# Two of every eight expert-row dot products through TensorE instead of VectorE

## What is computed

```
def peer(x, w_q, sub_keys, u_tab, v_tab):
    q = (xt @ w_q).reshape(n_tok, PEER_HEADS, 2, D_QHALF)
    sc = einsum("thcd,hckd->thck", q, sub_keys)
    top_s, top_i = top_k(sc, 16)                  # per head and half
    ...                                           # 16 x 16 pairs, best 16 of them
    experts, gates = ...                          # (tokens, 8 heads, 16)
    u = u_tab[experts]                            # 16384 rows of 2048 in each table
    h = einsum("thkd,td->thk", u, x)              # 128 dot products of 2048 per token
    coef = gates * gelu(h)
    return einsum("thk,thkd->td", coef, v_tab[experts])
```

## Time and profile before

| | us |
|---|---|
| median of 3 runs | 3703.89 |
| lowest, highest | 3697.67, 3709.7 |
| profiled execution | 3707.39 |
| its span, first to last instruction | 3705.7 |
| VectorE busy | 2809.0 (76%) |
| GpSimd busy | 2165.9 (58%) |
| TensorE busy | 2132.5 (58%) |
| ScalarE busy | 588.5 (16%) |
| mean granted TensorE clock | 0.769 of 2.4 GHz |
| HBM read | 1103.41 MB, 298 GB/s over the span |

### The profile page before, as it was taken

One profiled execution on the slowest core, in us unless ns is written; L12 is line 12 of the kernel. 1 busy time (PEld: TensorE's weight loads), 2 busy tenths in 40 slices (PEclk: granted clock), 3 DMA queues, 4 the chain that ended last, 5 costly groups with the idle time before them and its releaser, 6 DMA issues. The chain is left out here.

```text
span 3705.7 us, 32338 instructions
## 1 busy us (share of the span) xinstructions
PE 2132.5 (58%) x8985; PEld 1496.3 (40%) x8985; DVE 2809.0 (76%) x3476; ACT 588.5 (16%) x1079; POOL 2165.9 (58%) x1470
## 2 busy tenths in 40 slices
PE   8968890000111489999499998900001113799993
PEld 7855790000111354444297976900001113544441
DVE  4997589898999766666733545898989998666667
ACT  1002430000111430000033543300001113400000
POOL 6794175888777447767400001758787774477774
PEclk9987995555555589999799999955555555799997
DMA  7421447999999569999755334479999995599997
GB/s 242 143 84 62 142 149 306 395 409 381 422 421 419 201 231 410 408 409 403 291 201 183 126 126 148 145 304 392 412 364 418 422 420 220 210 404 407 409 407 299
DMA packets 293725, 1106.71 MB, mean 299 GB/s; under 512 B 21957, under 2 KB 120837, under 8 KB 220677
## 3 DMA queue, kind: packets, MB, share of 16 engines
q0 software_dynamic: 147456, 805.37, 54.4%
q1 hardware_dynamic: 146182, 300.22, 22.5%
HBM read 1103.41 MB, written 2.10 MB: 298 GB/s over the span
## 5 line engine op out<-in xcount | busy, mean ns | idle before, releaser
L1270 DVE SCALAR_TENSOR_TENSOR ring<-ring,x_tok 128x2048 f32<-128x2048 f32 x512 | 1147.7, 2288 | 56.8 <-DMA ring<-in_peer_u,index_now 53.3
L510 POOL DMA_INDIRECT ring<-in_peer_u,index_now x512 | 961.1, 1877 | 329.6 <-DVE ring L1270 152.9
L733 PE MATMUL ps<-all_v,mix 128*128 128x512 f32 x1984 | 851.8, 592 | 0.0
L531 POOL DMA_INDIRECT work<-in_peer_v,index_add x344 | 455.2, 1323 | 321.4 <-DVE x_tok L1294 174.7
L1294 DVE SCALAR_TENSOR_TENSOR x_tok<-work,coef,x_tok 128x1024 f32<-128x1024 f32 x344 | 441.6, 1286 | 240.2 <-DMA work<-in_peer_v,index_add 238.9
L733 PEld LDWEIGHTS ps<-all_v,mix 128*128 128x128 f32 x1984 | 377.0, 190 | 474.5 <-issue 474.5
L717 PE MATMUL ps<-hot,hot 128*128 128x128 f32 x1024 | 229.9, 411 | 568.2 <-ACT hot L928 568.1
L477 POOL TENSOR_TENSOR w_lo<-ring,w_hi 128x2048 fp32r<-128x2048 f32 x34 | 159.1, 4683 | 663.9 <-ACT w_hi L831 663.9
L717 PEld LDWEIGHTS ps<-hot,hot 128*128 128x128 f32 x1024 | 209.8, 311 | 588.5 <-ACT hot L928 588.5
L707 PE MATMUL ps<-ident,coef 128*128 128x128 f32 x4 | 1.9, 474 | 695.2 <-DVE coef L1288 695.2
L1103 DVE TENSOR_TENSOR w_lo<-ring,w_hi 128x2048 fp32r<-128x2048 f32 x78 | 178.8, 2292 | 264.8 <-ACT w_hi L831 264.8
(11 more groups left out here) (171 smaller groups left out, 2878.0 us busy)
## 6 DMA issues: line engine op xcount, KB each, us to landing
all_v<-in_peer_v SPq DMA_DIRECT2D x248, 512.0 KB, 6.7
ring<-in_conv_w_in SPq DMA_DIRECT2D x16, 2048.0 KB, 8.6
ring<-in_peer_w_q SPq DMA_DIRECT2D x16, 2048.0 KB, 8.3
ring<-in_attn_w_kv SPq DMA_DIRECT2D x16, 2048.0 KB, 8.3
ring<-in_conv_w_out SPq DMA_DIRECT2D x8, 2048.0 KB, 7.7
ring<-in_attn_w_q SPq DMA_DIRECT2D x8, 2048.0 KB, 8.4
ring<-in_attn_w_o SPq DMA_DIRECT2D x8, 2048.0 KB, 7.8
ring<-in_peer_u,index_now POOLq DMA_INDIRECT x512, 9.9
```

What stands on the lines that cost most here:

```text
L510: pool.indirect_dma_start(u_tile(s), None, u_tab, bass.IndirectOffsetOnAxis(ap=index_now[:, half, s:s + 1], axis=0)).then_inc(u_row[s], 16)
L531: pool.indirect_dma_start(add_tile(k), None, v_tab, bass.IndirectOffsetOnAxis(ap=index_add[:, half, k % TB, k // TB:k // TB + 1], axis=0)) ...
L733: mm = pe.matmul(ps[:, dense_bank(tb, q), :], mix[tb][:, row, :], tile[:, q * 512 - HALF:(q + 1) * 512 - HALF], start=False, stop=True, sk ...
L1270: dve.scalar_tensor_tensor(out=u_tile(s), in0=u_tile(s), scalar=1.0, in1=x_tok[:, tb, :], op0=ALU.mult, op1=ALU.mult, accum_out=coef[:, tb ...
```

## The change

In each group of eight tiles those in places 3 and 7 (`TURNED`) are no longer multiplied on VectorE. TensorE transposes such a tile in 16 blocks of 128 x 128, in two halves of two banks each (banks 4 to 7); ScalarE copies each half to `u_chan` in SBUF; TensorE then multiplies the 16 transposed blocks with the transposed x of the block (`x_dot`), summed into a 128 x 128 square of bank 2 or 3, whose diagonal holds the dot products; VectorE multiplies the square with the identity and sums (`take_dot`), one group later. `x_dot` is made once per block by 16 transposes and two copies. GpSimd's gather for places 3 and 7 now waits for `u_turned`, the transposes, and for the other six for `u_used` as before. The order of TensorE and ScalarE is rewritten so that the mixes of block 0 and the turned tiles of block 1 alternate; `turn_slots` moves from bank 2 to bank 0; the third v gather waits for the last product, as `x_dot` lies where `more_add` is.

```diff
+TURNED = (3, 7)
 ...
+        x_dot = nc.alloc_sbuf_tensor_at("x_dot", [P, KC, P], F32, offset=x_chan_at + 4 * 2048)
+        u_chan = view(18432, 2, KC // 2, P)
 ...  GpSimd
-                                        pool.wait_ge(u_used, i * (2 * U_RING) + ((base + half) * U_RING + s + 1))
+                                        if s in TURNED:
+                                            pool.wait_ge(u_turned, i * (4 * NT) + ((base + half) * (2 * NT) + 2 * TURNED.index(s) + 2))
+                                        else:
+                                            pool.wait_ge(u_used, i * (2 * ND) + ((base + half) * ND + DOTTED.index(s) + 1))
 ...
+                        if k == 2:
+                            pool.wait_ge(h_steps, 2 + 2 * NT * GROUPS * TB * (layer + 1))
 ...  TensorE
+                def turned_dots(tb, i):
+                    base = (layer * TB + tb) * GROUPS
+                    for e, s in enumerate(TURNED):
+                        n = base * NT + e
+                        pe.wait_ge(u_row[s], i * 16 + (base + 1) * 16)
+                        for h in range(2):
+                            pe.wait_ge(u_taken, i * (2 * NT) + (2 * n + h + 1))
+                            for c in range(KC // 2):
+                                k = h * (KC // 2) + c
+                                mm = pe.transpose(turned_banks(h)[:, c, :], u_tile(s)[:, k * P:(k + 1) * P], ident[:, :])
+                            mm.then_inc(u_turned, 1)
+                        pe.wait_ge(h_taken, i * NT + (n + 1))
+                        for h in range(2):
+                            pe.wait_ge(u_taken, i * (2 * NT) + (2 * n + h + 3))
+                            for c in range(KC // 2):
+                                mm = pe.matmul(ps[:, 2 + e, 0:P], u_chan[:, h, c, :], x_dot[:, h * (KC // 2) + c, :],
+                                               start=(h == 0 and c == 0), stop=(h == 1 and c == KC // 2 - 1), skip_group_check=True)
+                            mm.then_inc(h_steps, 1)
+
+                turn_dot_x(0)
+                with pe.Fori(0, GROUPS) as i:
+                    turned_dots(0, i)
+                turn_dot_x(1)
+                turned_dots(1, 0)
+                turn_slots(0)
+                turned_dots(1, 1)
+                with pe.Fori(0, GROUPS - 2) as i:
+                    mix_pair(0, i)
+                    turned_dots(1, i + 2)
+                with pe.Fori(GROUPS - 2, BATCHES // 2) as i:
+                    mix_pair(0, i)
 ...  ScalarE
+                def take_turned(tb, i):
+                    for e in range(NT):
+                        n = (layer * TB + tb) * GROUPS * NT + e
+                        for h in range(2):
+                            act.wait_ge(u_turned, i * (2 * NT) + (2 * NT + 2 * n + h + 1))
+                            act.wait_ge(h_steps, i * (2 * NT) + (2 * n + h + 1))
+                            act.activation(u_chan[:, h, :, :], turned_banks(h), ACT.Copy).then_inc(u_taken, 1)
 ...
+                take_dot_x(1)
+                take_turned(1, 0)
                 take_slots(0)
                 act.wait_ge(slot_taken, layer * TB + 1)
+                take_turned(1, 1)
+                with act.Fori(0, GROUPS - 2) as i:
+                    weigh_pair(i)
+                    take_turned(1, i + 2)
 ...  VectorE
+                def take_dot(tb, e, steps, slot):
+                    dve.wait_ge(h_steps, steps)
+                    block = ps[:, 2 + e, 0:P]
+                    dve.scalar_tensor_tensor(out=block, in0=block, scalar=1.0, in1=ident[:, :],
+                                             op0=ALU.mult, op1=ALU.mult, accum_out=coef[:, tb, slot]).then_inc(h_taken, 1)
+
                 def dots(tb, first, last):
                     base = (layer * TB + tb) * GROUPS
                     with dve.Fori(first, last) as i:
                         for s in range(U_RING):
-                            dot(tb, s, i * 16 + (base + 1) * 16, bass.ds(i * U_RING + s, 1))
+                            if s in TURNED:
+                                e = TURNED.index(s)
+                                take_dot(tb, e, i * (2 * NT) + (2 * ((base - 1) * NT + e) + 4), bass.ds(i * U_RING + s - U_RING, 1))
+                            else:
+                                dot(tb, s, i * 16 + (base + 1) * 16, bass.ds(i * U_RING + s, 1))
```

More of the change, by code:

```diff
@@ L62, in build @@
     GROUPS = SLOTS // U_RING
+    DOTTED = [s for s in range(U_RING) if s not in TURNED]
+    NT, ND = len(TURNED), len(DOTTED)
     HALF = D // 2
@@ L709, in mix_slots, with mix_pair @@
-                def mix_slots(tb):
+                    pe.transpose(ps[:, 0, 2 * P:3 * P], coef[:, tb, :], ident[:, :]).then_inc(slot_ready, 1)
+                def mix_pair(tb, i):
                     at = (layer * TB + tb) * BATCHES
[L712 to L718, removed]
@@ L720, in peer @@
-                for tb in range(TB):
-                    turn_slots(tb)
-                    mix_slots(tb)
+                    for b in range(2):
+                        pe.wait_ge(hot_ready, i * 2 + (at + b + 1))
+                        pe.wait_ge(mix_taken, i * 2 + (at + b + 1))
+                        for k in range(BATCH):
+                            mm = pe.matmul(ps[:, b, k * P:(k + 1) * P], hot_2[:, b, k, :], hot_1[:, b, k, :], start=True, stop=True)
+                        mm.then_inc(mix_ready, 1)
@@ L724, in peer @@
+                with pe.Fori(0, BATCHES // 2) as i:
+                    mix_pair(1, i)
                 for tb in range(TB):
@@ L930, in weigh_hot, with take_dot_x, weigh_pair @@
                     last.then_inc(hot_ready, 1)
-                exp_of(layer, 0, 1)
-                for half in range(2):
-                    exp_of(layer, 1, half)
+                def take_dot_x(tb):
+                    for h in range(2):
+                        act.wait_ge(dot_x_turned, 2 * (layer * TB + tb) + h + 1)
+                        act.activation(x_dot[:, h * (KC // 2):(h + 1) * (KC // 2), :], turned_banks(h), ACT.Copy).then_inc(dot_x_taken, 1)
+                def take_turned(tb, i):
+                    for e in range(NT):
+                        n = (layer * TB + tb) * GROUPS * NT + e
+                        for h in range(2):
+                            act.wait_ge(u_turned, i * (2 * NT) + (2 * NT + 2 * n + h + 1))
+                            act.sem_inc(act_tick, 1)
+                            act.wait_ge(h_steps, i * (2 * NT) + (2 * n + h + 1))
+                            act.sem_inc(act_tick, 1)
+                            act.activation(u_chan[:, h, :, :], turned_banks(h), ACT.Copy).then_inc(u_taken, 1)
+                take_dot_x(0)
+                exp_of(layer, 0, 1)
+                with act.Fori(0, GROUPS // 2) as i:
+                    take_turned(0, i)
+                exp_of(layer, 1, 0)
+                with act.Fori(GROUPS // 2, GROUPS) as i:
+                    take_turned(0, i)
+                exp_of(layer, 1, 1)
                 act.wait_ge(route[layer], part_at(1, 1) + PART_STEPS)
+                take_dot_x(1)
+                take_turned(1, 0)
                 take_slots(0)
                 act.wait_ge(slot_taken, layer * TB + 1)
+                take_turned(1, 1)
                 made = layer * TB * 2 * BATCHES
-                with act.Fori(0, BATCHES // 2) as i:
+                def weigh_pair(i):
                     for b in range(2):
@@ L946, in peer @@
                     take_mix(0, i, 1)
+                with act.Fori(0, GROUPS - 2) as i:
+                    weigh_pair(i)
+                    take_turned(1, i + 2)
+                with act.Fori(GROUPS - 2, BATCHES // 2) as i:
+                    weigh_pair(i)
                 take_slots(1)
@@ L1277, in dots, with last_dot, opening_dots @@
                         for s in range(U_RING):
-                            dot(tb, s, i * 16 + (base + 1) * 16, bass.ds(i * U_RING + s, 1))
-                def opening_dots(first, last):
+                            if s in TURNED:
[3 more added lines that the diff above has]
+                                dot(tb, s, i * 16 + (base + 1) * 16, bass.ds(i * U_RING + s, 1))
+                def last_dot(tb, e):
+                    s = TURNED[e]
+                    take_dot(tb, e, 2 * (((layer * TB + tb + 1) * GROUPS - 1) * NT + e) + 4, slice(SLOTS - U_RING + s, SLOTS - U_RING + s + 1))
+                def opening_dots(tb, first, last):
                     for s in range(first, last):
-                        dot(0, s, (layer * TB * GROUPS + 1) * 16, slice(s, s + 1))
+                        if s not in TURNED:
+                            dot(tb, s, ((layer * TB + tb) * GROUPS + 1) * 16, slice(s, s + 1))
+                        elif tb:
+                            last_dot(tb - 1, TURNED.index(s))
                 def weights(tb):
@@ L1325, in peer @@
                         dots(1, 2 + b // 2, 3 + b // 2)
+                for e in range(NT):
+                    last_dot(1, e)
```

35 lines of the change are left out of this document (25 added, 10 removed).

## The result

The changed kernel takes 3663.07 us, median of 4 runs (3659.05 to 3666.84); the kernel before took 3706.8 beside it. The ratio is 0.9877, with a 95% interval of 0.9859 to 0.9895: 1.2% faster. The forecast was 3673, the range of the forecast alone 3656 to 3692, and with the rivals 3648 to 3732. The measured difference is -43.7 us where -31 was forecast.

A forecast was written before the change was run, and what follows sets the result against it. Transfers nearly full, running dry in the first block behind GpSimd's late gathers. Terms -30 transfers, -4 start, -5 end, +6 TensorE, +2 seam make -31 us: 3676 against the profiled execution, 3673 on the median; range 3656 to 3692.

The forecast's parts named there:

- the copy as ninth slot: u stage: GpSimd's copy of eight indices takes another VectorE product's time (1.79 us), making nine products for eight gathers.
- (b): u stage, VectorE working through a backlog: products 2.21 us apart, GpSimd writes one gather per product, 1.91 us each.
- What the transfers give up: First gather after routing to last u gather, both layers: between 18 and 41 us gained, 30 taken.
- the start: Opening products of each layer go from four to three, so all that follows starts 2.2 us earlier: 4 us.
- VectorE's diagonals: 64 diagonals of 128x128 from PSUM a layer, 0.35 us each with accumulator read, 22 us a layer.
- 3 us of lag a layer: Second block: TensorE's added work puts groups 20.0 to 20.4 us apart; 3 us a layer charged, 6 in all.
- Rival 2: TensorE becomes the bound in the second block, groups over 20.4 us: 3732, or 3907 at 1.2 GHz throughout; chance 0.19.
- The stall at the seam: Between the blocks VectorE's weights wait for the gelu up to 6 us, covered by the ring; 2 us charged in all.
- The end of the stage: Last u gather to first mix of the next-to-last pair: 19.4 us instead of 21.7, 5 us gained in all.
- 9.9 to landing: End of the u stage: the last gather's tile was taken to land 9.9 us after issue.
- Rival 1: Transfers already at their limit through the uneven rate of scattered rows; gathers give 0 to 10 us, about 3698; chance 0.19.
- Rival 3: All 41 us of the transfers' gap gained and a fast end of the stage: 3650; chance 0.07.

## Why the prediction was right, point by point

**What bounds the kernel.** Right, and shown: GpSimd's one gather per product, the copy as ninth slot and the transfers running dry. Each of three ways to free GpSimd (one SBUF input less, no copy, fewer products) brought the first block from 396 to between 418 and 421 GB/s. The rule of the Trainium skill, "SBUF — State Buffer", section "Who interferes with whom", that stood beside (b) held.

**What the transfers give up.** Right mechanism, mis-sized: -30 in the sum, bounds 18 and 41; measured 21.3 + 26.3 = 47.6, outside the bounds. The upper bound took 2.484 us from a stretch of 13 products (whose rows give 29.78/12 = 2.482); the stage ran at 600.8/243 = 2.472 and 600.1/243 = 2.470, and 243 x 2 x 0.013 is the missing 6 us. And I stepped down from the bound to 30 for no row: nothing in the trace said that any of the gap would stay. Of the small terms, the start held: from the layer's first gather (550.63 before, 551.98 after) to the first one after the routing were 52.03 us in layer 0 and are 49.81, 2.2 less, and as much less in layer 1.

**VectorE's diagonals.** One takes 0.295 us and its accumulator read 0.141, but the read overlaps both neighbours: the next instruction starts 0.21 us after the diagonal (at 761.98 after 761.77), where 0.35 had been taken. VectorE is idle, as forecast, some 5 us in 20.

**TensorE.** A tile takes 7.15 us in the group shown, where 7.1 at full clock was worked out; but by luck, from two errors that cancel. The transposes came after a wait and took 3.48 us (1.97 in the run with doubled products, which left no wait), the products 3.83/32 = 0.12 us a pass instead of 0.145. Over all 128 tiles the transposes took 344.7/128 = 2.69 us and the products 539.5/128 = 4.21. The 0.145 was read from a short burst: 32 passes take 3.83 us and 64 take 7.41, which makes, as an estimate, 0.112 us a pass and 0.25 once per burst, and 1.15 for eight. The clock reached 0.83 to 0.91, not 0.75, and the 14 groups were 278.53/14 = 19.9 and 280.28/14 = 20.0 us apart, not 20.0 to 20.4 with 3 us of lag a layer: 6 us charged, none seen. Rival 2 falls for the change. The Trainium skill, "TensorE: Matmul & The Clock Gate", section "HAM oscillation — how this bites in real kernels", has each burst start slow after a wait; the transposes' 3.48 us in the group shown agree. But the products right behind them ran at full speed there (3.83 us); in layer 0's last tile they were slowed too (4.94).

**ScalarE.** Copies of 1.02 us (1.1 taken), hidden. The stall at the seam came as described: VectorE's gate multiplication at 925.48 waited 4.59 us for the gelu, and the stretch from 900 to 950 us still shows 1.01 and 421 GB/s. It was covered; the 2 us charged are not seen.

**The end of the stage.** Wrong in sign: -5 forecast, +2.8 measured by the same cut (from the last gather to the first mix 1226.21 - 1202.59 = 23.6 us in layer 0 and 3059.70 - 3037.12 = 22.6 in layer 1, against 21.7 in both before). The failed step is "9.9 to landing". That is the median of a kernel in which places came free late: even in its second block, where the transfers never ran dry, it is 11.0 (964 to 1225 us). In the changed kernel VectorE and TensorE wait for the tiles, a place is free soon after its tile has landed, and more gathers are on their way at once. The median is 14.4 us, and the last one took 1217.97 - 1202.59 = 15.4:

```profile
ring<-in_peer_u,index_now POOLq DMA_INDIRECT x512, 14.4
```

A gather that is issued earlier into a fuller queue lands later behind its issue. Counted from the issues, the transfers' gain is therefore a little too large and the end's loss makes up for it.

**The sum** by the prediction's own terms: -47.6 for the transfers (forecast -30), -4.4 for the start (-4), +2.8 for the end (-5), nothing for lag and seam (+8), and +3.4 us for the rest of the program (none forecast; 1.35 us of it lies ahead of the first gather of layer 0), together -45.8 (-31). So the forecast met the time more closely than it met its terms: transfers, start, lag and seam gave 26 us more than forecast, and the end and the rest of the program, which was put at nothing, took 11 of them back. Without that luck, the two as forecast, the time would have been about 3652, below the forecast's 3656. What made the 3.4 us of the rest stays open; 2.7 of them lie between layer 0's first mix and layer 1's first gather (1226.21 to 2387.01 us, before 1246.43 to 2404.53). Rival 1 falls: the missing 25 GB/s were no unevenness of scattered rows. Rival 3 names the transfers' gain best, but its fast end did not come; the time, 3663, lies between it and the forecast.

## What to carry to other kernels

If GpSimd writes gathers beside VectorE instructions with two SBUF inputs, count GpSimd's pieces of work per VectorE instruction, copies of indices included, before counting either engine's busy time; taking away one piece in nine, or one of the two SBUF inputs, brings most of what a quarter of VectorE's work brings. What a relieved engine can gain is bounded by the next limit, here the transfers: read it from the best stretch of the same trace, and do not step down from it without a row. A time from issue to landing is not a constant; it grows with the queue that the change itself fills (9.9 us before, 14.4 after).

## What the runs showed that was not expected

GpSimd's copy of 128 x 8 indices took 1.79 us beside a product with two SBUF inputs and 0.20 us beside one with an input in PSUM (means over a whole run 1.09 and 0.31); a gather 1.88 and 0.97 us on the mean. VectorE's product itself is as fast with x in PSUM as in SBUF (2281 and 2288 ns).

TensorE's clock rose to 0.83 to 0.91 with work in bursts of 7 us and waits of mostly 1 to 4 us between them, and an fp32 pass of 128 x 128 took 0.116 to 0.12 us at full clock.
